# Output projection in two parts, its weight rows asked for in another order, and one fold piece in each slot of the lead

## The reference, cut to what matters

```python
proj = rmsnorm(x) @ w_in                      # q, k, v, u of 512 columns each
attn = rmsnorm(diff_attention(q, k, v), subln_g) * 0.8
pool = concat([(window_mean(u_g) - u_g) @ pool_w[g] for g in range(4)]) * pool_scale
x1   = x + concat([attn, pool]) @ w_out       # (.,1024) @ (1024,1024)
xn   = rmsnorm(x1)
# PEER: 8 heads; per token and head the 16 best of 128*128 experts
s    = (xn @ wq) @ keys                       # folded: wqk = wq @ keys, once
h    = gelu(xn . u_tab[idx]);  x2 = x1 + sum(gate * h * v_tab[idx])
x3   = x2 + sigmoid(rmsnorm(x2) @ w_gate) * (p @ w_pl);  y = rmsnorm(x3)
```

## Time and profile before

| | |
|---|---|
| median of 3 runs | 3141.27 us (3138.45 to 3142.56) |
| the profiled execution, its own time | 3139.55 us |
| its span in the trace | 3137.3 us |
| PE, DVE, ACT, POOL busy | 74%, 71%, 30%, 42% of the span |
| moved by DMA | 1258.71 MB, 401 GB/s in the mean |
| of it by POOL's gathers | 1133.76 MB |

### The profile page before, as it was taken

How to read it: one execution, slowest core, us unless ns; L and a number is a source line. 1 busy time by engine, 2 the same in 40 slices (tenths; PEclk the granted TensorE clock), 3 DMA queues, 4 the chain that set the end, 5 groups by cost and what they waited for, 6 DMA issues and landing times.

```text
span 3137.3 us, 53529 instructions
## 1 busy us (share of the span) xinstructions
PE 2329.0 (74%) x21008; PEld 930.7 (30%) x21008; DVE 2219.7 (71%) x5418; ACT 953.2 (30%) x2437; POOL 1330.0 (42%) x1143
## 2 busy tenths in 40 slices
PE   8889998677877887757776667576777676677655
PEld 4643333233333333213432222122222222222112
DVE  1376767678868789656667667577777777777775
ACT  1422232335425345222322222132332332223222
POOL 1034444343444344345555544344444454444453
PEclk9999999788988888878978988798998897789877
DMA  7599999999999999999999999999999999999997
GB/s 275 210 391 421 420 410 421 417 408 391 404 401 418 409 394 419 417 408 417 416 417 411 416 417 404 418 403 420 406 419 410 420 415 421 395 420 420 420 415 314
DMA packets 201411, 1258.71 MB, mean 401 GB/s; under 512 B 24000, under 2 KB 27608, under 8 KB 60224
## 3 DMA queue, kind: packets, MB, share of 16 engines
q0 software_dynamic: 159808, 1133.76, 87.8%
q1 hardware_dynamic: 39916, 121.25, 9.9%
q10 hardware_dynamic: 1436, 0.29, 0.0%
HBM read 1226.74 MB, written 28.65 MB: 400 GB/s over the span
## 4 chain that ended last, share of the span: by engine, by line
DMA 31%; PE 14%; DVE 8%; POOL 3%; issue 3%; ACT 2%; DVEq 1%; another core or an unknown queue 0%; POOLq 0%; ACTq 0%
DMA ring<-in_uv,idx 31%; PE sc L1021 7%; DVE ring L1906 5%; PE sc L1054 3%; POOL ring L2128 2%; PE route L996 1%; PE sc L1023 1%; ACT diag L1428 1%; POOL front L2144 0%; DVEq L1916 0%; ACT hgelu L1423 0%; PE sc L718 0%; DVE x L1955 0%; PE sc L890 0%; PE sc L920 0%
## 5 line engine op out<-in xcount | busy, mean ns | idle before, releaser
L2128 POOL DMA_INDIRECT ring<-in_uv,idx x1056 | 1251.3, 1185 | 1623.8 <-PE sc L1023 1421.0
L1021 PE MATMUL sc<-ring,diag 32*32 32x512 f32 x8192 | 1237.8, 723 | 676.7 <-ACT diag L1428 616.5
L1906 DVE CUSTOM_DVE_ANT_0 ring<-ring,xn_cur 128x1024 f32<-128x1024 f32 x1056 | 1280.3, 1222 | 635.2 <-DMA ring<-in_uv,idx 583.5
L1023 PE MATMUL sc<-ring,diag 32*32 32x512 f32 x8192 | 1242.2, 723 | 0.0
L1021 PEld LDWEIGHTS sc<-ring,diag 32*32 32x32 f32 x8192 | 273.4, 117 | 1458.1 <-ACT diag L1428 1008.6
L1423 ACT ACTIVATE hgelu<-hdot 128x2 f32<-128x2 f32 x528 | 107.5, 204 | 1822.2 <-DVE hdot L1906 1753.2
L1428 ACT ACTIVATE diag<-gate_d,hgelu 128x32 f32<-128x32 f32 x1056 | 281.8, 314 | 21.2
L1023 PEld LDWEIGHTS sc<-ring,diag 32*32 32x32 f32 x8192 | 274.3, 117 | 4.7 <-issue 4.2
L578 PE MATMUL sc<-big,front 128*128 128x512 f32 x384 | 176.8, 603 | 2.5 <-DVE front L1535 1.6
L1423 ACT ACT_TABLE_LOAD x129 | 165.5, 1283 | 2.3
L996 PE MATMUL route<-big,xnT 128*128 128x256 f32 x560 | 135.4, 396 | 0.0
(11 more groups left out here) (310 smaller groups left out, 2277.5 us busy)
## 6 DMA issues: line engine op xcount, KB each, us to landing
front<-wqk_scratch SPq DMA_DIRECT2D x21, 1024.0 KB
ring<-in_uv,idx POOLq DMA_INDIRECT x1056
big<-in_w_in SPq DMA_DIRECT2D x8, 1024.0 KB, 13.8
wqk_scratch<-front SPq DMA_DIRECT2D x8, 1024.0 KB, 4.9
big<-wqk_scratch SPq DMA_DIRECT2D x8, 1024.0 KB, 20.6
x<-x_scratch SPq DMA_DIRECT2D x12, 512.0 KB
ring<-in_wq_t POOLq DMA_DIRECT2D x10, 512.0 KB, 13.9
front<-in_x SPq DMA_DIRECT2D x8, 512.0 KB
```

The source lines that it names most:

```text
L1021: pe.matmul(sc[own, 0, :], diag[own, r, :], uv_rows[own, place, D:D + W4], start=opens_sum, stop=closes).then_inc(row_added[r], 1)
L1023: pe.matmul(sc[other, 1, :], diag[own, r, :], uv_rows[own, place, D + W4:2 * D], start=opens_sum, stop=closes).then_inc(row_added[r], 1)
L1906: dve.tensor_tensor_reduce(uv_rows[:, row_of(k), 0:D], uv_rows[:, row_of(k), 0:D], xn_cur[:, :], 1.0, 0.0, ALU.mult, ALU.add, hdot[:, n % ...
L2128: pool.indirect_dma_start(uv_rows[:, row_of(k), :], None, uv, bass.IndirectOffsetOnAxis(ap=idx[:, n % PH, j:j + 1], axis=0)).then_inc(row_ ...
```

## The change

Three things are changed.

1. `out(t, c)` becomes `out_pooled(t, c)`, k = 4 to 7, which opens the bank, and `out_heads(t, c)`, k = 0 to 3, which closes it. For tiles 2 to 7 the pooled parts go to slots e+1 and e+2, in front of `add_rows` of those slots. For tile 0 they go to slots -8 and -7, for tile 1 they stay beside the heads' parts. Matmuls, sizes and sums are the same in number.
2. The row blocks of `w_out` are loaded in the order 4, 5, 6, 7, 0, 1, 2, 3, with a semaphore for each half. In the lead SP asks for a block in the slot of the fold itself, ahead of the store. `wq_st` is turned round by four blocks with it.
3. `fold_slot` has pieces 9, 10, 11, 12 in slots -8, -7, -6, -6 instead of -9, -8, -7, -6, and piece 13 in -5 instead of -6.

```diff
-    return -LEAD + (1, 2, 3, 4, 5, 6, 7, 8, 9, 9, 10, 11, 12, 12, 13, 15)[j]
+    return -LEAD + (1, 2, 3, 4, 5, 6, 7, 8, 9, 10, 11, 12, 12, 13, 13, 15)[j]
...
+POOLED_0 = (ATT[0].heads, ATT[0].out[0])
...
+def pooled_slot(t, c):
+
+    a = ATT[t]
+    return (POOLED_0[c], a.out[c])[t] if t < EARLY else a.norm[c]
...
-                return cut(ring_a, j * D, D)
+                return cut(ring_a, w_out_after(j) * D, D)
...
+        def w_out_after(j):
+
+            return (j + H) % KD
...
-            def out(t, c):
+            def out_pooled(t, c):
...
                 if c == 0:
-                    pe.wait_ge(w_out_in, 16 * KD if t < EARLY else 16 * 2 * KD)
+                    pe.wait_ge(w_out_in[1], 16 * H if t < EARLY else 16 * 2 * H)
                     w = band_bank(t)
                     pe.wait_ge(free[w], emptied(w, ("pool", t)))
+                pe.wait_ge(free[b], opens(b, ("out", t, c)))
+                for k in range(H, KD):
+                    pe.matmul(bank[b], a.xT[:, k, :], a.wo[:, k, c * W4:(c + 1) * W4], start=(k == H), stop=False)
+
+            def out_heads(t, c):
+
+                a = B[t]
+                b = (S0, S1)[c]
+                if c == 0:
+                    pe.wait_ge(w_out_in[0], 16 * H if t < EARLY else 16 * 2 * H)
                     pe.wait_ge(free[TA], emptied(TA, ("heads", t)))
-                pe.wait_ge(free[b], opens(b, ("out", t, c)))
-                for k in range(KD):
-                    mm = pe.matmul(bank[b], a.xT[:, k, :], a.wo[:, k, c * W4:(c + 1) * W4],
-                                   start=(k == 0), stop=(k == KD - 1))
+                for k in range(H):
+                    mm = pe.matmul(bank[b], a.xT[:, k, :], a.wo[:, k, c * W4:(c + 1) * W4], start=False, stop=(k == H - 1))
                 mm.then_inc(ready[b], 1)
...
+                    if t == 0 and s == pooled_slot(0, 0):
+                        out_pooled(0, 0)
                     if s == a.heads:
                         turn_out(t)
...
+                        if s == pooled_slot(t, c) and (t, c) != (0, 0):
+                            out_pooled(t, c)
                         if s == a.out[c]:
-                            out(t, c)
+                            out_heads(t, c)
...
-                        load_rows(B[EARLY].wo, w_out, k, w_out_in)
+                        load_rows(B[EARLY].wo, w_out, w_out_after(k), w_out_in[w_out_after(k) // H])
...
+                for j in range(KD):
+                    if s == fold_slot(j):
+                        sp.wait_ge(ready[A1], filled(A1, ("fold", j)))
+                        load_rows(B[0].wo, w_out, w_out_after(j), w_out_in[w_out_after(j) // H])
                 for i, hd in enumerate(FOLD_HEADS):
...
-                for k in range(KD):
-                    if s == fold_slot(k) + 1:
-                        sp.wait_ge(ready[A1], filled(A1, ("fold", k)))
-                        load_rows(B[0].wo, w_out, k, w_out_in)
```

More of the change, by code:

```diff
@@ L433, in front_and_experts @@
         w_in_in = [sem(f"w_in_in{k}") for k in range(KD)]
-        w_out_in = sem("w_out_in")
+        w_out_in = [sem(f"w_out_in_{n}") for n in ("heads", "pooled")]
         x_in = [sem(f"x_in{i}") for i in range(2)]
```

## The result

The changed kernel takes 3124.3 us (median of 6 runs, 3122.1 to 3127.3), the kernel before, run beside it on the same chip, 3141.9 us (6 runs). The ratio is 0.9948, with a 95% interval from 0.9938 to 0.9958: faster by 17.5 us, where 18 were forecast. A second series of the same kernel, on another chip, gave 3124.35 against 3141.1 us (0.9949, 0.9935 to 0.9962). The profiled execution took 3122.1 us, its span is 3120.0.

What follows compares the result with a forecast made beforehand. Transfers, nearly all gathers, set the main part's pace; the lead and dips at the outputs lose time. 3139.55 - 10.1 (lead) - 8 (outputs) = 3121.4, plus 1.7 for a median: 3123 us, range 3113 to 3133.

Steps and rivals of the forecast that it cites:

- The lead: Time before the first gather at 161.70 us: forecast to shorten by 10.1 us, bounds 5 and 11.3.
- The four losses: PE from piece 8 to `out(0, 1)`: 2.88 hole, 1.48 slow piece 9, 4.42 `w_out` wait, 2.48 slow output; 11.3 us.
- the new wait for ACT: Lead, fold pieces 12 and 14 behind the norm: 2.1 us of waiting instead of 1.08, so 1.0 us more.
- The slow rows: Lead: piece 9 takes 1.48 us more and the output half after the `w_out` wait 2.48 more, at PE's lower clock.
- Rival C: Lead: heads' blocks of `w_out` come late, PE waits at the heads' half; lead wins about 5 us, 3128; chance 0.07.
- The main part: Outputs of tiles 2 to 7: no slot has over a quarter product, dips vanish; 8 us gained, bounds 0 and 12.9 plus 4.
- the DMA share: Seven windows dipping at outputs: 1.01 less each window's share, counted as time the engines stood, 8.9 us in sum.
- DVE's waits for the product: Outputs over all tiles: six waits of DVE for PE, 17.8 us, forecast to go nearly all.
- rival B: Main part: lead is won, but dips only move to e+1 and e+2, DVE's share being high; 3131; chance 0.19.
- The signs: Trace checks: 128x512 passes at median 592 ns, output windows at 410 GB/s and above, first gather near 151.6 us.
- Two signs of failure: Main part: prediction wrong if dipping windows are merely others (e+1, e+2), or 128x512 passes above 1000 ns appear.
- rival D: Main part: quarter outputs run at the lower clock, 3.4 us more for each of 24; slower, 3166; chance 0.03.

Runs made afterwards that it cites:

- The run that only asks early: Kernel before with tiles 2 to 7 split and `w_out` blocks requested earlier, old fold slots, tile 0's output whole: fold piece 8 to first gather 49.95 us.
- the run of the main part only: Kernel before with only the pooled parts of tiles 2 to 7 moved to e+1 and e+2, old lead order: 3134.6 us, ratio 0.9985.
- the whole-output run: Changed kernel with tile 2's output written in one piece at its old slots, tiles 3 to 7 still split: 3125.0 us, ratio 0.9945.
- the run with the shorter maximum: Changed kernel with tile 3's largest score taken from the first 128 of 512 columns of each map: 3123.0 us, ratio 0.9943.

## Why the prediction was right, point by point

**The lead: forecast 10.1, measured 11.1.** The four losses were the right ones (11.3 in sum). PE's output half stood directly behind piece 8, at 103.75 where 105.2 was forecast (1.26 of it the start by chance), there was no wait for `w_out`, and the first gather began at 149.32, with the start by chance added 150.6, forecast 151.6. The term that was mis-sized is the new wait for ACT, 1.0: the wait of 1.08 us moved to piece 12 as forecast, and the second, at piece 14, is 0.29 us. My way of laying ACT's copies end to end made it too large. The slow rows (1.48 and 2.48) were counted in full. The run that only asks early shows that the first of them does not always follow the hole; before and in the run of the main part only it did (3.50, 3.59). Without that row's slowness the lead before would have been 1.5 us shorter, so part of the 11.1 is not sure to be there in every execution.

The clock rose with it. The window from 120 to 125 us stood at 0.52. The same in the changed kernel:

```profile
120.00:125.00 5.00, 5.00 (x25) 3.09 (x24) 0.69 (x1) 1.48 (x4) 0.00 (x0) 1.00 0.34 105
```

**Rival C did not come.** There was no wait for the heads' blocks; with the pieces in other slots there was none even with the late request.

**The main part: forecast 8, measured 4.5 to 5.6** (slot 210 of the table in three traces; 5.2 by the medians of the run with this half alone). The term that was mis-sized is the gain of 8 us for the outputs, which takes the DMA share that the dips lack as time won at every tile. The reasoning was that PE's load fits its slot and DVE's waits go, and the dips with them: the first two are right, the last only in part. DVE's waits for the product (17.8 us) are gone from the changed kernel's list of the main part. In their place DVE waits for the transfers, 82 us from 661 to 1300 us where it was 60:

```profile
DVE ring L1929 <- DMA ring<-in_uv,idx: 82.0, 64, 3.7
```

```profile
DVE ring L1906 <- DMA ring<-in_uv,idx: 60.0, 51, 2.8
```

By tile, from the same three traces: tile 2 0.0 to -0.3 (the whole-output run: at most 0.8), tile 3 2.4 to 3.6, tile 4 2.5, tile 5 1.1 to 1.8, tile 6 -0.3 to 0.6, tile 7 -0.7 to -1.5. By the DMA share I had 1.2, 1.7, 2.0, 1.4 and 2.6 for tiles 2 to 6. Tiles 3, 4 and 5 are better than forecast, 6.2 to 7.1 us for 5.1; tiles 2, 6 and 7 are where the sum fails, 3.8 forecast and 0.1 to 2.2 lost. The stretches of scores differ in DVE's share. In the changed kernel, from the outputs of tiles 2 to 6 through the scores behind them, in turn:

```profile
690.00:740.00 50.00, 36.55 (x325) 14.96 (x325) 46.83 (x119) 27.98 (x59) 16.33 (x16) 0.80 0.92 367
780.00:840.00 60.00, 44.82 (x424) 20.66 (x423) 51.21 (x131) 27.52 (x67) 26.27 (x22) 0.86 1.01 421
900.00:960.00 60.00, 41.07 (x402) 16.77 (x400) 52.24 (x119) 31.88 (x66) 24.44 (x21) 0.83 0.99 409
1030.00:1090.00 60.00, 43.12 (x434) 16.69 (x440) 49.82 (x119) 32.01 (x66) 22.30 (x22) 0.84 1.01 417
1160.00:1230.00 70.00, 46.35 (x492) 19.86 (x492) 62.58 (x143) 38.44 (x78) 27.56 (x24) 0.91 1.00 408
```

DVE is busy for 94% of the first and 89% of the last, and for 85, 87 and 83% of those between. For tile 2 the run with the shorter maximum shows that the stretch behind it is limited by DVE's work on the scores or by the chain from the maximum to ACT: what PE is late by at the output then hardly counts, because the transfers fall behind at the scores anyway. That this is all of it is not shown: with the scores spread, which eases DVE, the split of tile 2 still won nothing by slot 104. For tiles 6 and 7 the same cause is only argued, from DVE's share and the window at 1190 us; no run took work from DVE there, windows with DVE at 9.4 and 9.6 of 10 us carry 418 and 422 GB/s, and the loss of about 1 us at tile 7 stays open. The row that should have told me was in the same table as the dips: rival B named DVE's high share behind the outputs, and I put it against the whole gain instead of against each tile. For tile 2 it came true. I also read that table wrong in one place: PE is busy 10 of 10 us in five of the seven windows, not in four, which speaks a little more for rival B than I gave it.

**The signs.** The passes of 128x512 have the forecast median of 592 ns at both lines. Two signs of failure did appear. Of the windows that dip now, those at 1120 and 1240 us stand at e+1 and e+2 of tiles 6 and 7, where the pooled parts went, and just behind; at the other tiles the windows there carry 413 GB/s and more. And there is a pass over 1000 ns in the main part, with one of 951 ns behind it; together they are worth about 1 us, and the heads' part has a mean of 613 ns against 603 over 96 rows.

```profile
L728 PE MATMUL sc<-big,front x96: 592/592/697, 640.3 to 1246.8; 128*128 128x512 f32 x96
...
L738 PE MATMUL sc<-big,front x96: 592/592/1222, 663.3 to 1265.5; 128*128 128x512 f32 x96
```

The pass is the first of tile 2's heads' part, at 663.3 us. PE had waited 2.61 us for ACT up to 660.58, and the granted clock then was 0.50, the lower level:

```profile
662.00:664.00 2.00, 2.00 (x17) 0.50 (x2) 1.30 (x3) 0.00 (x0) 1.13 (x2) 0.50 1.05 427
```

The rule of the Trainium skill (TensorE: Matmul & The Clock Gate, HAM oscillation — how this bites in real kernels) that short bursts between waits fall to the lower clock agrees with the output and the fold pieces behind the holes of the lead, with one exception (2.02 us behind 2.88 us of waiting). The quarter outputs of the main part did not follow it, but for that one. So rival D stayed away.

**The sum.** 18.1 forecast, 17.5 and 16.8 measured in two series. Part of the agreement is luck: two misses of opposite sign, the lead forecast 1.0 too low and the main part about 3 too high. The range was wide enough for that, and rival B's 3131 would have been the answer had tiles 3 to 5 gone as tile 2.

## What to carry to other kernels

A dip in the rate of the transfers is not by itself time to be won: filling one was worth 2.4 to 3.6 us at tiles 3 and 4 and at most 0.8 us at tile 2, where the stretch behind it was itself limited. Count the gain dip by dip, and read the busy share of each engine behind each dip; a high share is a warning and no proof (9.6 of 10 us stood beside full transfers too). A hole in a dependent chain, with a named releaser, was worth its length here and that of the slow rows behind it, and it was filled by work whose inputs were old. Where several edits remove the same wait, each alone may do: try them apart before counting their gains together.

## What was unexpected

- The lead repeats to 0.01 us between chips (47.36 or 47.37 us from fold piece 8 to the first gather in all eight traces that have it), while the time ahead of it differs by 2.3 us between traces (piece 8 at 101.70 to 104.03). A gain of a few us in a fixed chain is better read from two events in the trace than from medians.
- The same 2.88 us hole was followed by a fold piece of 3.50 and 3.59 us in two profiles and of 2.02 us in another. The granted clock from 105 to 110 us was 0.77 before and 0.81 with the main part only, and 1.00 in the third. What decides it was not found.
- In the stretch of tile 3's scores, 3.2 us of DVE's work taken away gave 2.5 to 2.8 us by slot 96, though POOL's waits there name PE.
